# Three whole sums of squares split into two rounded products each, and an earlier wait for the first query transfers

## The chip, the cores and the metric

The kernel runs on one core of one Trainium2 chip. The time is the device time of one execution in microseconds (us), from launch to completion, and the figure used is the median of several runs. One further execution was taken with the hardware profiler: it gives each engine's instructions in time. The engines named here are TensorE (PE, matrix products; its weight loads are listed as PEld), VectorE (DVE), ScalarE (ACT), GpSimd (POOL) and SyncE (SP, which issues nearly all transfers).

## The reference, cut to what matters

Two layers work on a sequence of 512 tokens of width 1024. The first is a gated short convolution with an MLP, the second is attention with a forget gate and an MLP. The change touches the attention layer, where every key head and every query head (64 wide) is divided by its root mean square.

```python
def rms_norm(x, g):
    xf = x.astype(jnp.float32)
    y = xf * lax.rsqrt(jnp.mean(xf * xf, axis=-1, keepdims=True) + EPS)
    return y.astype(x.dtype) * g

def shared_kv(x, kv_norm_g, w_kv, k_norm_g, w_f, b_f):
    h = rms_norm(x, kv_norm_g)
    k, v = jnp.split(h @ w_kv, 2, axis=-1)
    k = rms_norm(k.reshape(b, s, N_HEADS, HEAD_DIM), k_norm_g)
    ...

def fox_mixer(h, q_w, q_norm_g, o_w, k, v, F):
    q = rms_norm((h @ q_w).reshape(b, s, N_HEADS, HEAD_DIM), q_norm_g)
    ...
        logits = jnp.einsum("bqhd,bkhd->bhqk", qb, k).astype(jnp.float32) * scale
        logits = logits + (Fq[..., :, None] - F[..., None, :])
        ...
        p = jax.nn.softmax(logits, axis=-1)
        return jnp.einsum("bhqk,bkhd->bqhd", p.astype(v.dtype), v)
```

## The kernel before

**Tiles and formats.** Activations lie with the features on the 128 partitions and the 512 tokens along the row. Keys, values and queries come in eight blocks of 128 features each (two heads per block), named k0 to k7, v0 to v7 and q0 to q7. A product with dense weights is made of three: each operand is split into a rounded part (`_hi`, type fp32r) and the rest (`_lo`), and hi·hi, lo·hi and hi·lo are added in one bank (lines 609 to 611). One block is 8 such triples over the 8 input tiles. ACT writes the rounded part of each weight block (`w_hi`, line 1117), DVE the rest (`w_lo`, line 1543). `after_block` queues both steps for the weight block three places further on.

**The order is written out by hand.** Each engine has its own list of calls, and semaphores tie them together. On every engine an instruction that waits holds up all behind it. The blocks come in the order k0, v0, k1, q0, q1, v1, and from then on k, q, v of each further number. PE alternates pieces of blocks (`kvq`) with the sums of squares (`head_sum`), the turns of values (`v_turn`), and the steps of attention: `logits`, `turn_probs`, `output`.

**The norm of one head block**, for example of k1, runs over three engines:

1. ACT, `head_square`: squares the finished bank into `tb` (line 1379), in slot 1, for q0 in slot 0.
2. PE, `head_sum`: a product with `ones_head` gives the mean over 64 features. For the blocks in `WHOLE_SQUARES` (k0, q0, k1, q1) it is one product of the whole float32 square, which the profile shows as two instructions (line 915). For all others ACT first writes a rounded copy `sq_hi` (line 1383), DVE writes the rest `sq_lo` over the square (`square_low`, line 2002), and PE multiplies the two parts (lines 918 and 920).
3. ACT, `head_root`: three activations (lines 1395 to 1397) on the sum.
4. DVE, `head_norm`: three instructions (lines 1988, 1996, 1997). The first reads the sum's bank and signals `hn_read`, the third writes the normed block `ty` and signals `normed`.
5. ACT `high` and DVE `low` split it into `qk` (lines 1402 and 2007), and SP copies that to `keys` or `queries` (line 457), from where `logits` reads.

**What else stands nearby.** The sums of k0, k1 and q1 and the turned values of block 0 share bank 3, so PE waits for `hn_read` of k1 before it starts the sum of q1. ACT's list after the first key block is: `high` of k0, square of k1, weights, square of q0, `v_high(0)` (line 1416, rounded values), root of q0, `high` of q0, root of k1, square of q1, two weight blocks, and the exponentials of head 0. DVE's list there is: norm of k0, rest of four query input tiles (`g_lo`, line 1590), weights, `low` of k0, `v_low(0)`, weights, norm of q0, `low` of q0, norm of k1, two weight blocks, and the maxima of head 0.

## Time and profile before

| | us |
|---|---|
| median of 3 runs | 1198.12 |
| lowest and highest | 1197.79, 1198.91 |
| the profiled execution, device time | 1198.92 |
| its span, first to last instruction | 1197.1 |
| PE busy in that span | 1179.0 (98%) |
| DVE busy | 763.2 (64%) |
| ACT busy | 499.5 (42%) |

The profile lists instructions with start and duration, and in brackets the idle time before one and what ended it. Matmuls are pipelined, so a matmul's listed duration is longer than the distance to the next one; what it costs PE is read from the distance between starts. The granted clock of PE is 0.999 of full speed over the span. The part that the change touches lies between about 589 and 637 us.

### The profile page before, as it was taken

How to read it: one execution, taken by the hardware profiler on the slowest of the kernel's cores; microseconds unless marked ns; L12 is line 12 of the kernel's file. 1: busy time of each engine (PE TensorE's matmuls, PEld its weight loads, DVE VectorE, ACT ScalarE, POOL GpSimd, SP SyncE). 2: the span in 40 equal slices, each digit the busy share in tenths (PEclk: the TensorE clock that was granted, in tenths of full speed). 3: DMA queues.
4: the chain of work that ended last, by engine and by line, in shares of the span. 5: the costliest groups of instructions: out<-in, count | busy, mean ns of one | idle time of the engine just before them, and what ended most of it. 6: DMA issues, size and time to landing. Idle time of an engine off the chain costs nothing.

```text
span 1197.1 us, 17104 instructions
## 1 busy us (share of the span) xinstructions
PE 1179.0 (98%) x5899; PEld 989.9 (83%) x5899; DVE 763.2 (64%) x1119; ACT 499.5 (42%) x815; POOL 24.4 (2%) x37
## 2 busy tenths in 40 slices
PE   6999999999999999999999999999999999999998
PEld 4788889888888888889978888889888888888887
DVE  5656888875665665555979898986743443443442
ACT  5422332542332332333767778864531331331431
POOL 2000000000000000002010000000000000000000
PEclk9999999999999999999999999999999999999999
DMA  9767654576666565332355544441333333333333
GB/s 335 230 194 245 189 177 132 156 237 192 187 206 196 174 200 166 88 91 71 89 141 136 130 107 124 122 127 52 90 90 103 90 104 89 104 91 101 91 102 89
DMA packets 228642, 168.77 MB, mean 141 GB/s; under 512 B 5636, under 2 KB 210604, under 8 KB 228588
## 3 DMA queue, kind: packets, MB, share of 16 engines
q1 hardware_dynamic: 228396, 167.92, 48.0%
q8 instruction: 34, 0.56, 0.2%
q0 software_dynamic: 32, 0.07, 0.0%
q14 instruction: 20, 0.16, 0.0%
q10 hardware_dynamic: 160, 0.06, 0.0%
HBM read 153.24 MB, written 2.10 MB: 130 GB/s over the span
## 4 chain that ended last, share of the span: by engine, by line
PE 90%; DVE 6%; ACT 1%; issue 1%; SPq 1%; DMA 1%; DVEq 0%; ACTq 0%
PE bank L609 28%; PE bank L611 28%; PE bank L610 28%; PE bank L956 1%; PE bank L974 1%; PE bank L707 1%; PE bank L946 1%; DVE w_lo L1543 1%; DMA first_raw<-in_sc_w_in 1%; PE bank L947 1%; DVE neg_max L2022 1%; SPq L385 1%; PE bank L737 0%; DVE h_lo L1592 0%; DVE probs L2035 0%
## 5 line engine op out<-in xcount | busy, mean ns | idle before, releaser
L609 PE MATMUL bank<-h_hi,w_hi 128*128 128x512 f32 (+1 forms) x864 | 326.2, 378 | 2.0 <-issue 1.1
L611 PE MATMUL bank<-h_hi,w_lo 128*128 128x512 f32 (+1 forms) x864 | 322.7, 373 | 0.0
L610 PE MATMUL bank<-h_lo,w_hi 128*128 128x512 f32 (+1 forms) x864 | 322.6, 373 | 0.0
L1117 ACT ACTIVATE w_hi<-raw 128x1024 fp32r<-128x1024 f32 x184 | 193.3, 1054 | 259.6 <-DMA raw<-in_mlp_w 222.3
L609 PE MATMUL bank<-g_hi,w_hi 128*128 128x512 f32 (+1 forms) x696 | 261.8, 376 | 0.0
L611 PE MATMUL bank<-g_hi,w_lo 128*128 128x512 f32 (+1 forms) x696 | 259.2, 372 | 0.0
L610 PE MATMUL bank<-g_lo,w_hi 128*128 128x512 f32 (+1 forms) x696 | 259.0, 372 | 0.0
L1543 DVE TENSOR_TENSOR w_lo<-raw,w_hi 128x1024 fp32r<-128x1024 f32 x184 | 224.7, 1224 | 45.7 <-ACT w_hi L1117 42.7
L609 PEld LDWEIGHTS bank<-h_hi,w_hi 128*128 128x128 f32 x864 | 162.6, 188 | 32.7 <-issue 3.2
L610 PEld LDWEIGHTS bank<-h_lo,w_hi 128*128 128x128 f32 x864 | 162.7, 188 | 28.7 <-issue 0.5
L611 PEld LDWEIGHTS bank<-h_hi,w_lo 128*128 128x128 f32 x864 | 162.6, 188 | 28.8
L610 PEld LDWEIGHTS bank<-g_lo,w_hi 128*128 128x128 f32 x696 | 131.2, 188 | 23.1 <-issue 0.5
L611 PEld LDWEIGHTS bank<-g_hi,w_lo 128*128 128x128 f32 x696 | 131.1, 188 | 22.9
L609 PEld LDWEIGHTS bank<-g_hi,w_hi 128*128 128x128 f32 x696 | 131.1, 188 | 22.6 <-issue 0.5
L1851 DVE SCALAR_TENSOR_TENSOR x<-bank,mod,x 128x512 f32 (+1 forms) x63 | 47.2, 750 | 141.1 <-PE bank L611 139.7
L1903 DVE TENSOR_TENSOR tb<-ta 128x512 f32<-128x512 f32 x64 | 44.3, 691 | 127.6 <-ACT ta L1319 127.6
L1319 ACT ACTIVATE ta<-bank 128x512 f32<-128x512 f32 x64 | 38.2, 596 | 195.8 <-PE bank L611 195.8
L1806 DVE SCALAR_TENSOR_TENSOR ada_acc<-ada_raw,c_act,ada_acc 128x1024 f32 (+1 forms) x80 | 102.2, 1277 | 0.6 <-DVE ada_acc L1806 0.2
L1907 DVE TENSOR_TENSOR g_lo<-tb,g_hi 128x512 f32 (+1 forms) x64 | 44.3, 693 | 15.0 <-ACT g_hi L1321 12.4
L1321 ACT ACTIVATE g_hi<-ta 128x512 f32 x64 | 40.5, 634 | 8.1
L1428 ACT ACTIVATE probs<-bank,neg_max 128x512 f32<-128x512 f32 (+1 forms) x64 | 32.9, 525 | 21.8 <-DVE neg_max L2022 21.1
L1138 ACT ACTIVATE tb<-x 128x512 f32<-128x512 f32 x15 | 9.5, 632 | 55.5 <-DVE x L1851 49.7
(225 smaller groups left out, 1072.1 us busy)
## 6 DMA issues: line engine op xcount, KB each, us to landing
raw<-in_mlp_w SPq DMA_DIRECT2D x128, 512.0 KB, 4.1
ada_raw<-in_ada_w SPq DMA_DIRECT2D x40, 1024.0 KB, 5.6
raw<-in_sc_w_in SPq DMA_DIRECT2D x20, 512.0 KB, 4.4
ada_first<-in_ada_w SPq DMA_DIRECT2D x32, 256.0 KB, 7.9
raw<-in_w_kv SPq DMA_DIRECT2D x16, 512.0 KB, 3.9
raw<-in_sc_w_out SPq DMA_DIRECT2D x8, 512.0 KB, 3.9
raw<-in_q_w SPq DMA_DIRECT2D x8, 512.0 KB, 4.7
keys<-qk SPq DMA_DIRECT2D x16, 256.0 KB, 3.1
```

Source lines behind the costliest of these rows:

```text
L609: mm(out[:, cols], weights_hi, hi[:, k, cols], start=(k == 0), stop=False)
L610: mm(out[:, cols], weights_hi, lo[:, k, cols], start=False, stop=False)
L611: return mm(out[:, cols], weights_lo, hi[:, k, cols], start=False, stop=(k == KT - 1))
L1117: go(w_hi[:, jj, :, :], raw[:, jj, :, :], ACT.Copy).then_inc(hi_ok, 1)
L1319: go(ta[:, jj % 2, :], bank[jj][:], ACT.Relu).then_inc(bank_free, 1)
L1321: go(tile3(g_hi, j), ta[:, jj % 2, :], ACT.Square).then_inc(g_hi_ok, 1)
L1428: go(probs[:, P_OFF[qt]:P_OFF[qt] + n], bank[at_bank][:, c0:c0 + n], ACT.Exp, bias=neg_max[:, s:s + 1], accum_out=p_sum[:, s:s + 1]).then_ ...
L1543: tt(w_lo[:, jj, :, :], raw[:, jj, :, :], w_hi[:, jj, :, :], ALU.subtract).then_inc(lo_ok, 1)
L1806: stt(out=acc, in0=ada_raw[:, s, half * D:(half + 1) * D], scalar=col(c_act, k), in1=acc, op0=ALU.mult, op1=ALU.add).then_inc(ada_used, 1)
L1851: stt(out=tile3(x, j), in0=bank[jj][:], scalar=mcol(layer, part, j), in1=tile3(x, j), op0=ALU.mult, op1=ALU.add).then_inc(bank_free, 1)
L1903: tt(tb[:, s, :], ta[:, s, :], ta[:, s, :], ALU.mult).then_inc(g_a, 1)
L1907: tt(tile3(g_lo, j), tb[:, s, :], tile3(g_hi, j), ALU.subtract).then_inc(g_ok, 1)
```

## The change

Only q0 stays in `WHOLE_SQUARES`. The squares of k0, k1 and q1 are now split as all later ones: ACT writes a rounded copy, DVE the rest, PE multiplies two parts. The copy of k0 goes to a new place, `first_sq_hi` in slot 0 of `tb`, as the usual place still holds query input; so the copy of the values into that slot waits for the sum of k0. The sum of k0 moves on PE from inside block v0 to its end. On ACT `v_high(0)` moves ahead of the square of q0, and in the last pair of the loop all four exponentials of head 13 stand ahead of `high` of q7, where before two stood ahead and two behind. On SP the first copy of each query half waits for the rounded part (`q_hi_ok`) alone; only the second copy waits for the rest (`q_ok`).

```diff
@@ -71,7 +71,7 @@
 SUM_BANK["q", 0] = 5
 SUM_BANK.update({("q", j): 7 for j in range(2, KT)})
 SQUARE_SLOT = {name: 0 if name == ("q", 0) else 1 for name in KVQ_ORDER}
-WHOLE_SQUARES = (("k", 0), ("q", 0), ("k", 1), ("q", 1))
+WHOLE_SQUARES = (("q", 0),)
 PARTS_OF = {name: n for n, name in enumerate(name for name in NORM_ORDER if name not in WHOLE_SQUARES)}
 
 
@@ -171,6 +171,7 @@
     qk, = stacked(region_qk, [("qk", [P, 2, 2, T], F32R)])
     region_tb = region(size([P, 2, T], F32))
     tb, = stacked(region_tb, [("tb", [P, 2, T], F32)])
+    first_sq_hi, = stacked(region_tb, [("first_sq_hi", [P, T], F32R)])
     sq_lo, = stacked(region_tb + size([P, T], F32), [("sq_lo", [P, T], F32R)])
     region_tc = region(size([P, 2, T], F32))
     tc, = stacked(region_tc, [("tc", [P, 2, T], F32)])
@@ -206,6 +207,9 @@
     def mcol(layer, part, j):
         k = (layer * NMOD + part) * KT
         return mod[:, k + j:k + j + 1] if isinstance(j, int) else mod[:, bass.ds(j + k, 1)]
+
+    def high_square(kind, j):
+        return first_sq_hi[:] if (kind, j) == ("k", 0) else sq_hi[:]
 
     def kv_gain(j):
         return cols[:, R_KV + j:R_KV + j + 1]
@@ -478,10 +482,11 @@
             def head_queries(j, half):
 
                 own, other, h = OWN[half], OWN[1 - half], 2 * j + half
-                sp.wait_ge(q_ok, j + 1)
+                sp.wait_ge(q_hi_ok, j + 1)
                 if j:
                     sp.wait_ge(s_ok, TT * (h - 1))
                 copy(queries[own, :, half, :], qk[own, 0:1, 0, :].broadcast_to([HD, 2, T])).then_inc(queries_in[half], 16)
+                sp.wait_ge(q_ok, j + 1)
                 copy(queries[other, 0, half, :], qk[own, 1, 0, :]).then_inc(queries_in[half], 16)
 
             def rest_of_pair(j):
@@ -915,7 +920,7 @@
                     mm(out, ones_head[:].bitcast(F32), tb[:, SQUARE_SLOT[kind, j], :], start=True, stop=True).then_inc(hn_pe, 1)
                 else:
                     pe.wait_ge(hn_hi, PARTS_OF[kind, j] + 1)
-                    mm(out, ones_head[:], sq_hi[:], start=True, stop=False)
+                    mm(out, ones_head[:], high_square(kind, j), start=True, stop=False)
                     pe.wait_ge(hn_lo, PARTS_OF[kind, j] + 1)
                     mm(out, ones_head[:], sq_lo[:], start=False, stop=True).then_inc(hn_pe, 1)
 
@@ -988,9 +993,8 @@
                                 block_target(KVQ, bank[KVQ_BANK["k", 0]])], 2,
                          (BLOCK_OF["v", 0], bank[KVQ_BANK["v", 0]]))
             pe.wait_ge(bank_free, KVQ)
-            kvq("v", 0, range(0, 6), cols=HALF[1])
+            kvq("v", 0, range(KT), cols=HALF[1])
             head_sum("k", 0)
-            kvq("v", 0, range(6, KT), cols=HALF[1])
             kvq("k", 1, range(KT))
             pe.wait_ge(fg_act, 2)
             kvq("q", 0, EARLY, lambda k: pe.wait_ge(h_ok, H_Q + k + 1))
@@ -1379,8 +1383,9 @@
                 go(tb[:, SQUARE_SLOT[kind, j], :], bank[KVQ_BANK[kind, j]][:], ACT.Square).then_inc(hn_sq, 1)
                 if (kind, j) not in WHOLE_SQUARES:
                     act.wait_ge(hn_sq, SQUARE_OF[kind, j] + 1)
-                    act.wait_ge(hn_pe, NORM_OF[kind, j])
-                    go(sq_hi[:], tb[:, SQUARE_SLOT[kind, j], :], ACT.Copy).then_inc(hn_hi, 1)
+                    if (kind, j) != ("k", 0):
+                        act.wait_ge(hn_pe, NORM_OF[kind, j] if (kind, j) != ("k", 1) else NORM_OF["k", 0] + 1)
+                    go(high_square(kind, j), tb[:, SQUARE_SLOT[kind, j], :], ACT.Copy).then_inc(hn_hi, 1)
 
             def root_of(kind):
                 return (tc[:, 0, :], ty[:, 0, :]) if kind == "q" else (tv[:], ty[:, 1, :])
@@ -1403,8 +1408,8 @@
 
             def v_copy(j):
                 act.wait_ge(pe_done, BLOCK_OF["v", j] + 1)
-                if j == 1:
-                    act.wait_ge(hn_pe, NORM_OF["q", 0] + 1)
+                if j < 2:
+                    act.wait_ge(hn_pe, NORM_OF["kq"[j], 0] + 1)
                 if j:
                     act.wait_ge(v_turned, j)
                 go(tb[:, 0, :], bank[KVQ_BANK["v", j]][:], ACT.Copy).then_inc(v_copied, 1)
@@ -1466,8 +1471,8 @@
             high("k", 0)
             head_square("k", 1)
             after_block("k", 1)
+            v_high(0)
             head_square("q", 0)
-            v_high(0)
             head_root("q", 0)
             high("q", 0)
             head_root("k", 1)
@@ -1498,9 +1503,10 @@
                 after_block("q", nxt)
                 head_root("q", nxt)
                 v_copy(nxt)
-                exponentials(2 * i + 1, 0, 2)
+                exponentials(2 * i + 1, 0, 2 if nxt < KT - 1 else TT)
                 high("q", nxt)
-                exponentials(2 * i + 1, 2, TT)
+                if nxt < KT - 1:
+                    exponentials(2 * i + 1, 2, TT)
                 out_high(2 * i)
                 if nxt < KT - 1:
                     head_square("k", nxt + 1)
@@ -1999,7 +2005,7 @@
 
             def square_low(kind, j):
                 dve.wait_ge(hn_hi, PARTS_OF[kind, j] + 1)
-                tt(sq_lo[:], tb[:, 1, :], sq_hi[:], ALU.subtract).then_inc(hn_lo, 1)
+                tt(sq_lo[:], tb[:, 1, :], high_square(kind, j), ALU.subtract).then_inc(hn_lo, 1)
 
             def low(kind, j):
                 n = "qk".index(kind)
@@ -2057,6 +2063,7 @@
             query_tile(2)
             query_low(1)
             query_tile(3)
+            square_low("k", 0)
             query_low(2)
             query_low(3)
             after_block("k", 0)
@@ -2071,11 +2078,13 @@
                 query_low(j)
             after_block("v", 0)
             low("k", 0)
+            square_low("k", 1)
             v_low(0)
             after_block("k", 1)
             head_norm("q", 0)
             low("q", 0)
             head_norm("k", 1)
+            square_low("q", 1)
             after_block("q", 0)
             after_block("q", 1)
             maxima(0)
```

ACT, from `high` of k0 on (`qk`) to the root of q0 (`bank5`); `tb<-bank7` is the square of k1, `tb<-bank0` that of q0, and `v_parts` is `v_high(0)`. Before:

```order
L1402 ACTIVATE qk_91<-ty_90 128x512
L1379 ACTIVATE tb_92<-bank7 128x512
L1117 ACTIVATE w_hi_82<-raw_83 128x1024
L1379 ACTIVATE tb_92<-bank0 128x512
L1416 ACTIVATE v_parts_103<-bank3 128x4x2x64
L1395 ACTIVATE ty_90<-bank5,eps_col_115 128x512
```

The same place after the change:

```order
L1407 ACTIVATE qk_91<-ty_90 128x512
L1383 ACTIVATE tb_92<-bank7 128x512
L1388 ACTIVATE sq_hi_96<-tb_92 128x512
L1121 ACTIVATE w_hi_82<-raw_83 128x1024
L1421 ACTIVATE v_parts_104<-bank3 128x4x2x64
L1383 ACTIVATE tb_92<-bank0 128x512
L1400 ACTIVATE ty_90<-bank5,eps_col_116 128x512
```

Two instructions have come in ahead of the square of q0: the rounded copy of k1's square, and the rounded values, which stood behind it.

DVE, from the last instruction of q0's norm to the maxima of head 0. Before:

```order
L1997 SCALAR_TENSOR_TENSOR ty_90<-bank0,q_gain_113,ssum_88 128x512
L2007 TENSOR_TENSOR qk_91<-ty_90,qk_91 128x512
L1988 SCALAR_TENSOR_TENSOR ssum_88<-bank3,tv_96 128x512
L1996 SCALAR_TENSOR_TENSOR ssum_88<-ssum_88,ty_90 128x512
L1997 SCALAR_TENSOR_TENSOR ty_90<-bank7,k_gain_114,ssum_88 128x512
L1543 TENSOR_TENSOR w_lo_81<-raw_83,w_hi_82 128x1024 x2
L2022 TENSOR_REDUCE neg_max_118<-bank6 128x1
```

The same place after the change:

```order
L2003 SCALAR_TENSOR_TENSOR ty_90<-bank0,q_gain_114,ssum_88 128x512
L2013 TENSOR_TENSOR qk_91<-ty_90,qk_91 128x512
L1994 SCALAR_TENSOR_TENSOR ssum_88<-bank3,tv_97 128x512
L2002 SCALAR_TENSOR_TENSOR ssum_88<-ssum_88,ty_90 128x512
L2003 SCALAR_TENSOR_TENSOR ty_90<-bank7,k_gain_115,ssum_88 128x512
L2008 TENSOR_TENSOR sq_lo_94<-tb_92,sq_hi_96 128x512
L1549 TENSOR_TENSOR w_lo_81<-raw_83,w_hi_82 128x1024 x2
L2028 TENSOR_REDUCE neg_max_119<-bank6 128x1
```

The rest of q1's square (`sq_lo`) stands behind all three instructions of k1's norm.

PE, the sum of q1 inside block v1 (`bank0`) and the start of the first logits (`mask_b`). Before:

```order
L611 MATMUL bank0<-h_hi_50,w_lo_81 128x512
L915 MATMUL bank3<-tb_92,ones_head_100 128x512
L609 MATMUL bank0<-h_hi_50,w_hi_82 128x512
L610 MATMUL bank0<-h_lo_51,w_hi_82 128x512
L611 MATMUL bank0<-h_hi_50,w_lo_81 128x512
L936 MATMUL bank6<-mask_b_102,ident_b_101 128x128
```

The same place after the change:

```order
L616 MATMUL bank0<-h_hi_50,w_lo_81 128x512
L923 MATMUL bank3<-sq_hi_96,ones_head_101 128x512
L925 MATMUL bank3<-sq_lo_94,ones_head_101 128x512
L614 MATMUL bank0<-h_hi_50,w_hi_82 128x512
L615 MATMUL bank0<-h_lo_51,w_hi_82 128x512
L616 MATMUL bank0<-h_hi_50,w_lo_81 128x512
L941 MATMUL bank6<-mask_b_103,ident_b_102 128x128
```

The sum stands at the same place, now as two products, of which the second needs DVE's `sq_lo`.

## Rows read from the trace of the kernel before

**Rows 1.** The page: the chain of waits that ended last, by engine

```profile
PE 90%; DVE 6%; ACT 1%; issue 1%; SPq 1%; DMA 1%; DVEq 0%; ACTq 0%
```

**Rows 2.** Chain of waits in order of time, sums of squares: start, us, what

```profile
591.51 0.86 PE bank L915 x2
...
609.02 0.86 PE bank L915 x2
...
660.80 0.23 PE bank L918
```

**Rows 3.** Timeline of ACT, `high` of k0 to `v_high(0)`: start, duration, what

```profile
601.16 0.63 ACT L1402 ACTIVATE qk<-ty 128x512 fp32r<-128x512 f32 x1 [1.21 <-DVE g_lo L1590]
601.69 0.58 ACT L1379 ACTIVATE tb<-bank 128x512 f32<-128x512 f32 x1
602.17 1.05 ACT L1117 ACTIVATE w_hi<-raw 128x1024 fp32r<-128x1024 f32 x1
604.51 0.60 ACT L1379 ACTIVATE tb<-bank 128x512 f32<-128x512 f32 x1 [1.28 <-PE bank L611]
605.00 0.59 ACT L1416 ACTIVATE v_parts<-bank 128x512 fp32r<-128x512 f32 x1
```

**Rows 4.** Timeline of ACT, the square of k2 with its rounded copy

```profile
630.09 0.58 ACT L1379 ACTIVATE tb<-bank 128x512 f32<-128x512 f32 x1
630.70 0.63 ACT L1383 ACTIVATE sq_hi<-tb 128x512 fp32r<-128x512 f32 x1
631.23 0.57 ACT L1446 ACTIVATE o_hi<-bank 64x512 fp32r<-64x512 f32 x1
```

**Rows 5.** Timeline of PE, the sum of q0 and the product ahead of it

```profile
604.76 0.39 PE L611 MATMUL bank<-g_hi,w_lo 128*128 128x512 f32 x1
605.16 1.12 PE L915 MATMUL bank<-tb,ones_head 128*128 128x512 f32 x2
```

**Rows 6.** Timeline of DVE, the norm of k1 to the maxima of head 0

```profile
613.18 0.69 DVE L1988 SCALAR_TENSOR_TENSOR ssum<-bank,tv 128x512 f32<-128x512 f32 x1 [1.21 <-ACT tv L1397]
613.91 0.69 DVE L1996 SCALAR_TENSOR_TENSOR ssum<-ssum,ty 128x512 f32<-128x512 f32 x1
614.64 0.75 DVE L1997 SCALAR_TENSOR_TENSOR ty<-bank,k_gain,ssum 128x512 f32<-128x512 f32 x1
615.31 2.35 DVE L1543 TENSOR_TENSOR w_lo<-raw,w_hi 128x1024 fp32r<-128x1024 f32 x2
617.57 1.67 DVE L2022 TENSOR_REDUCE neg_max<-bank 128x1 f32<-128x512 f32 x4
```

**Rows 7.** Timeline of DVE, the rest of the square of k2 and what follows

```profile
631.61 0.68 DVE L2002 TENSOR_TENSOR sq_lo<-tb,sq_hi 128x512 fp32r<-128x512 f32 x1
632.22 0.68 DVE L2049 TENSOR_TENSOR o_lo<-bank,o_hi 64x512 fp32r<-64x512 f32 x1
```

**Rows 8.** Timeline of PE, the sum of q1 to the first logits

```profile
613.62 0.39 PE L611 MATMUL bank<-h_hi,w_lo 128*128 128x512 f32 x1
613.93 1.12 PE L915 MATMUL bank<-tb,ones_head 128*128 128x512 f32 x2
...
615.12 0.40 PE L610 MATMUL bank<-h_lo,w_hi 128*128 128x512 f32 x1
...
615.60 0.40 PE L936 MATMUL bank<-mask_b,ident_b 128*128 128x128 bf16 x4
616.11 0.47 PE L946 MATMUL bank<-keys,queries 128*128 128x512 f32 x1
```

**Rows 9.** Timeline of SP, the copies of the first queries: issue, duration, what

```profile
612.00 2.74 SPq L457 DMA_DIRECT2D queries<-qk  x4
```

**Rows 10.** Stretches: length, PE busy (instructions), granted clock, DMA share, GB/s

```profile
20.00:24.00 4.00, 3.45 (x16) 0.69 1.08 361
24.00:28.00 4.00, 4.00 (x21) 0.88 1.11 349
```

**Rows 11.** Timeline of PE, the product after the longest wait between products

```profile
20.55 1.06 PE L727 MATMUL bank<-ident,x_unit 128*128 128x128 f32 x8 [1.78 <-ACT tc L1224]
```

## The prediction, on record before the changed kernel ran

> **What bounds the kernel now.** I read the chain of waits first. PE has 90% of it and DVE 6% [rows 1], so time is won or lost where PE's list gets shorter or where PE has to wait. The change touches only the stretch from the first key block to the first logits, and one place near the end of attention. For that stretch I then read the timelines of PE, ACT, DVE and SP side by side. The reader is to see three things. The sums of squares stand in an unbroken row of products, so a shorter sum is time won if its inputs are there [rows 2]. ACT is idle for 1.21 and 1.28 us just ahead of the steps that feed q0's sum [rows 3], which is room for added work, but not for all of it. And the sum of q1 already starts late, since PE waits for the first instruction of k1's norm, with two more of that norm behind it on DVE [rows 6, 8].
>
> **What the split sums save on PE.** In an unbroken row the float32 sum costs 0.86 us (k0 and k1) and one rounded product 0.23 [rows 2]. Two of these are 0.46, so each of k0, k1 and q1 saves 0.40 to 0.41, in all 1.2 us. After an idle moment the float32 pair costs more: from 613.93 to 615.12 less the 0.23 of the one product between, 0.96 [rows 8]. Moving k0's sum from inside v0 to its end adds no product.
>
> The row says that a float32 product costs 0.86/0.23 = 3.7 rounded ones. The Trainium skill (FP8 and Floating Point Precision, TensorE Precision Notes) counts four passes through the array for true float32. By four passes the three sums would save 0.46 each, 1.4 us in all, against the 1.2 by the rows.
>
> **k0: the added work is covered, but it pushes ACT and DVE.** A square with its copy takes ACT 631.23 − 630.09 = 1.14 us, a square alone 602.17 − 601.69 = 0.48 [rows 3, 4], so each copy adds 0.66 to ACT's list. Each `sq_lo` adds 632.22 − 631.61 = 0.61 to DVE's [rows 7]. The sum of k0 now stands some 0.7 us later on PE, where copy and rest are done. But ACT and DVE have no pause from there to `high` of k0, which waits for DVE's `g_lo` [rows 3]. DVE in turn waits for ACT's root of k0. So `high` of k0 starts 0.66 later, at 601.82; PE does not wait for it.
>
> **q0: ACT's backlog reaches the sum.** From 601.82 on ACT runs `high`, the square of k1, its copy (0.66 again), a weight block and now `v_high(0)`. The weight block starts at 602.17 + 0.66 + 0.66 = 603.49 and passes the engine on 0.95 later (an instruction starts about 0.1 before the listed end of the last one), at 604.44. `v_high(0)` takes 0.49, taken from the distance 604.51 to 605.00 of the square there [rows 3]. The square of q0 starts at 604.93 and lasts 0.60, to 605.53. With the 0.05 from square to product of before (604.51 + 0.60 = 605.11, then 605.16) the sum of q0 starts at 605.58 [rows 3, 5]. Before, it started at 605.16, after a wait of 605.16 − (604.76 + 0.23) = 0.17 [rows 5]. PE, 0.41 earlier through k0, would be ready at 604.58, so the wait grows from 0.17 to 1.0: **+0.83**. The move of `v_high` costs 0.49 of that: without the copies it would fit into the idle 1.28, with them it does not. The gain of k0 is gone, and PE stands 0.42 later than before.
>
> **k1.** Its copy ends near 603.6 (601.82, then 0.53 for `high`, 0.61 for the square, 0.63 for the copy), and its `sq_lo` follows on DVE. PE comes to the sum at 605.58 + 0.96 + 4 tiles of three products (2.7) = 609.3, so the parts are long there. So its 0.41 is won, and PE is level with before (613.8) when it comes to the sum of q1.
>
> **q1: a new wait.** Between the sum of q0 and that of q1 runs a chain that the change leaves as it is: root of q0 on ACT, norm of q0 on DVE, `high` of q0 and root of k1 on ACT, first instruction of k1's norm on DVE. It took 613.93 − 605.16 = 8.77 us [rows 5, 8]. So PE may start the sum of q1 at 605.58 + 8.77 = 614.35. The first product needs ACT's copy. The second needs `sq_lo`, and on DVE that stands behind the second and third instruction of k1's norm. Before, the instruction in that place (the weights) started at 615.31 [rows 6]; 0.42 later is 615.73, and with 0.68 for the subtraction [rows 7] it ends at 616.41. PE goes on at 616.45 and is through at 616.68. Before it was through at 615.12 − 0.23 = 614.89 [rows 8]. **PE is 1.8 us behind here**, of which 1.46 is pure waiting between the two products. Queued behind the second product are the rest of v1 and the logits of head 0; no other engine has work that would shorten this. Behind `sq_lo` on DVE stand two weight blocks and the maxima of head 0. These were not waiting for PE before (DVE came without a pause, at 617.57 [rows 6]); they come about 1.0 later (0.42 + 0.61), and PE's logits 1.5 later, so DVE adds nothing.
>
> **Queries.** Four products of 128 columns need about 0.23, so before the first logits PE waited (616.11 − 615.60) − 0.23 = 0.28 [rows 8], most likely for the query copies issued from 612.00 [rows 9]. Now the first copy needs only the rounded part, which comes 0.42 later but spares the rest (0.68): the copies go out about 0.3 earlier, and PE comes 1.8 later. The wait goes: **−0.3**. For later blocks I take zero: the copies land while PE has other work. Bounds: −0.3 to 0.
>
> **The last pair.** Head 13's last two exponentials now stand ahead of `high` of q7. On ACT that place was idle, waiting for DVE's norm of q7, and DVE's own order is unchanged, so I take zero. No row tells it better; by one exponential and half a wait the bounds are −0.4 to +0.4.
>
> **Sum against the profiled span.** −0.41 (k0) + 0.83 (q0) − 0.41 (k1) + 1.8 (q1, with its own saving) − 0.3 (queries) = +1.5 us, so the span goes from 1197.1 to 1198.6. After the first logits PE is the bound again and carries this to the end. The profiled execution took 1198.92, 0.8 above the median; against the median, 1198.12 + 1.5 = 1199.6.
>
> **Rivals.**
>
> *Cover holds.* If the parts of q1's square are there when PE comes, and q0's square is on time, only savings are left: −1.23, the waits of 0.17 ahead of q0 and 0.08 ahead of q1 (613.93 − 613.62 − 0.23) [rows 8], and 0.28 for the queries, −1.7: 1196.4. For it: the room of 1.21 and 1.28 on ACT [rows 3]. Against it: DVE's order, in which `sq_lo` of q1 cannot start before k1's norm is over. Chance 0.10.
>
> *q0 on time, q1 late.* If ACT catches up by the square of q0 (less than 0.5 of backlog), PE comes to it as early as it can. Square and sum then start 0.41 earlier than before, and all of the q1 chain with them: 0.8 less than my forecast, +0.7, 1198.8. Chance 0.15.
>
> *The clock falls (slower).* After its longest wait between products, 1.78 us with one-column products ahead of it, PE's granted clock was 0.69 in 20 to 24 and 0.88 in 24 to 28 [rows 10, 11]. That is 4 × 0.31 + 4 × 0.12 = 1.7 us lost at the 1.2 GHz level. The change makes PE idle for nearly all of 614.0 to 616.45, with one product in it. If that is enough, the loss is 1.5 + 1.7 = 3.2: 1201.3. It decides when the wait at q1 is at least as long as the one at 20 us. Against it: the products right before and after are full 512-column ones. Chance 0.17.
>
> The Trainium skill (TensorE: Matmul & The Clock Gate, HAM oscillation) tells of the same fall after idle gaps between bursts of products. The trace agrees once, in the rows just named.
>
> *It does nothing.* If savings and waits cancel, the time is 1198.1. I count that between the second rival and the forecast, chance 0.03.
>
> **How the numbers follow.** The forecast, 1199.0 to 1200.4 with the bounds of the small terms, has 0.55. With the second rival and the clock the range 1197.8 to 1201.6 holds about 0.87; what is left out is the case of cover and accidents. About 0.2% (2.4 us) is what a measurement of this kernel can tell from no change. Faster than 1195.7 needs more than every saving together: 0.03. Slower than 1200.5 needs the clock or the upper end of the forecast: 0.17 + 0.06 = 0.23. The rest is within 0.2%: 0.74.
>
> **What would show it.** In the changed profile: two products of 0.23 at k0 with no idle before them; the square of q0 on ACT starting at 604.9 without idle before it; the sum of q0 at 605.6; q1's second product more than 1.5 us behind the first, with DVE's `sq_lo` as releaser; first logits near 617.6; clock 1.00 from 612 to 620. I am wrong if ACT is idle ahead of q0's square, if DVE does `sq_lo` of q1 before k1's norm ends, or if waits after 620 us shrink and give the 1.5 back.

## The result: 1200.9 us, 0.2% slower than before

| | us |
|---|---|
| before, median of 20 runs beside the changed kernel | 1198.24 (1197.50 to 1200.03) |
| after, median of 20 runs | 1200.90 (1199.43 to 1202.64) |
| after / before, with 95% interval | 1.0023 [1.0017, 1.0029] |
| after, span of the profiled execution | 1200.8 |

The kernel became 2.7 us slower, where 1.5 was forecast. The 20 runs are spread wide, and their mean granted clocks tell why in part: 7 runs have a mean clock of 0.996 and take 1201.95 to 1202.64 (median 1202.53). The other 13 have 0.997 to 0.999 and a median of 1200.42. Of 87 runs of the kernel before, taken beside this kernel's experiments, none has a mean clock of 0.996. The profiled execution of after is one of the 7. Its span is 3.7 longer than that of before.

Of these 3.7, about 0.6 arose before anything that the change touches. ACT's square of k0 starts at 589.39 before and at 589.96 after. In the profiled executions of this case it lies anywhere between 588.25 and 589.96. A part of that goes with the granted clock near the start, which in 16 to 28 us is 0.72 in some executions (after and five others: square at 589.24 to 589.96) and 0.86 in the rest (before and six others: 588.25 to 589.39). Where single times of after are compared with before, I take off 0.58 (instructions ahead of the change start 0.57 to 0.59 apart). For whole stretches I count from that square of k0.

**k0 and k1.** The sums cost PE what two rounded products cost in a row, without an idle moment. This timeline of PE (start, duration, what, and in brackets the idle time before it and what ended it) answers to the first two of [rows 2]:

```profile
592.63 0.40 PE L923 MATMUL bank<-first_sq_hi,ones_head 128*128 128x512 f32 x1
592.87 0.40 PE L925 MATMUL bank<-sq_lo,ones_head 128*128 128x512 f32 x1
593.10 0.39 PE L614 MATMUL bank<-h_hi,w_hi 128*128 128x512 f32 x1
...
609.86 0.39 PE L923 MATMUL bank<-sq_hi,ones_head 128*128 128x512 f32 x1
610.09 0.39 PE L925 MATMUL bank<-sq_lo,ones_head 128*128 128x512 f32 x1
```

From 592.63 to 593.10 are 0.47, and at k1 the two are 0.23 apart, 0.46 for both. Before it was 0.86 each.

**q0.** ACT has no pause between `high` of k0 and the square of q0, and PE waits for that square. First ACT, as [rows 3], then PE, as [rows 5]:

```profile
602.40 0.63 ACT L1407 ACTIVATE qk<-ty 128x512 fp32r<-128x512 f32 x1 [1.21 <-DVE g_lo L1596]
602.94 0.58 ACT L1383 ACTIVATE tb<-bank 128x512 f32<-128x512 f32 x1
603.55 0.63 ACT L1388 ACTIVATE sq_hi<-tb 128x512 fp32r<-128x512 f32 x1
604.09 1.05 ACT L1121 ACTIVATE w_hi<-raw 128x1024 fp32r<-128x1024 f32 x1
605.04 0.58 ACT L1421 ACTIVATE v_parts<-bank 128x512 fp32r<-128x512 f32 x1
605.51 0.59 ACT L1383 ACTIVATE tb<-bank 128x512 f32<-128x512 f32 x1
```

```profile
604.93 0.39 PE L616 MATMUL bank<-g_hi,w_lo 128*128 128x512 f32 x1
606.15 1.13 PE L920 MATMUL bank<-tb,ones_head 128*128 128x512 f32 x2 [0.84 <-ACT tb L1383]
```

The product ahead is through at 604.93 + 0.23 = 605.16, so the wait is 0.99, where [rows 5] give 0.17.

**q1.** PE waits twice. The timeline of PE answers to [rows 8]:

```profile
614.17 0.39 PE L616 MATMUL bank<-h_hi,w_lo 128*128 128x512 f32 x1
615.45 0.47 PE L923 MATMUL bank<-sq_hi,ones_head 128*128 128x512 f32 x1 [0.90 <-ACT sq_hi L1388]
617.05 0.80 PE L925 MATMUL bank<-sq_lo,ones_head 128*128 128x512 f32 x1 [1.13 <-DVE sq_lo L2008]
617.64 0.63 PE L614 MATMUL bank<-h_hi,w_hi 128*128 128x512 f32 x1
618.07 0.63 PE L615 MATMUL bank<-h_lo,w_hi 128*128 128x512 f32 x1
...
618.93 0.65 PE L941 MATMUL bank<-mask_b,ident_b 128*128 128x128 bf16 x4
619.34 0.78 PE L951 MATMUL bank<-keys,queries 128*128 128x512 f32 x1
```

The waits are 1.05 ahead of the first product and nearly all of the 1.60 between the two. On DVE the rest of the square stands where the prediction put it, behind the whole norm of k1 (as [rows 6]):

```profile
614.19 0.69 DVE L1994 SCALAR_TENSOR_TENSOR ssum<-bank,tv 128x512 f32<-128x512 f32 x1 [1.21 <-ACT tv L1402]
...
615.65 0.75 DVE L2003 SCALAR_TENSOR_TENSOR ty<-bank,k_gain,ssum 128x512 f32<-128x512 f32 x1
616.32 0.68 DVE L2008 TENSOR_TENSOR sq_lo<-tb,sq_hi 128x512 fp32r<-128x512 f32 x1
616.91 2.35 DVE L1549 TENSOR_TENSOR w_lo<-raw,w_hi 128x1024 fp32r<-128x1024 f32 x2
620.49 1.68 DVE L2028 TENSOR_REDUCE neg_max<-bank 128x1 f32<-128x512 f32 x4 [1.23 <-PE bank L952]
```

**The clock.** From 617.64 on the products stand 0.43 apart instead of 0.23. The granted clock in stretches of 1 us (length, PE busy with instructions, clock, DMA share, GB/s) shows it:

```profile
616.00:617.00 1.00, 0.00 (x0) 0.91 0.99 245
617.00:618.00 1.00, 0.95 (x2) 0.50 0.65 180
618.00:619.00 1.00, 1.00 (x4) 0.50 1.10 334
619.00:620.00 1.00, 1.00 (x7) 0.50 0.14 42
620.00:621.00 1.00, 1.00 (x7) 0.89 0.00 0
```

0.50 is the 1.2 GHz level. Near the end of the second wait, the clock fell, and it was back some 3.4 us later (finer stretches give 0.53 for 616.8 to 617.0, 0.50 from there to 620.2, and 0.94 for the 0.2 us behind). The 0.09 that is missing in the first row passed while PE had nothing to do, so what PE lost is 3 × 0.50 + 0.11 = 1.6 us. Before, 612 to 624 has a granted clock of 1.00.

From the square of k0 to the turn of the fourth block of probabilities there are 66.66 us before and 69.75 after: 3.1 more. Less the 1.6 for the clock, 1.5 is left for waits and savings.

### The profile page after: what moved, and what is told of

Same layout as the page of the kernel before. It is cut to its first block, busy times and chain, and to the rows that moved or that the text cites. A ratio compares the mean times of both kernels' runs of the same rounds, so it can differ in the third digit from the quotient of the medians.

```text
span 1200.8 us, 17113 instructions
## 1 busy us (share of the span) xinstructions
PE 1179.6 (98%) x5899; PEld 991.8 (83%) x5899; DVE 765.4 (64%) x1122; ACT 501.7 (42%) x818; POOL 24.7 (2%) x37
## 4 chain that ended last, share of the span: by engine, by line
PE 90%; DVE 5%; ACT 2%; issue 1%; SPq 1%; DMA 1%; DVEq 0%; ACTq 0%
PE bank L614 28%; PE bank L616 27%; PE bank L615 27%; PE bank L961 1%; PE bank L979 1%; PE bank L951 1%; PE bank L952 1%; PE bank L712 1%; DMA first_raw<-in_sc_w_in 1%; SPq L389 1%; DVE h_lo L1598 0%; DVE w_lo L1549 0%; PE bank L742 0%; DVE tc L1589 0%; DVE x L1628 0%
```

## The experiments

Each was run 11 times beside 27 to 33 runs of the kernel before (medians 1198.31, 1198.34 and 1198.31), except the queries alone, which have one execution. The stretch is that from ACT's square of k0 to the turn of the fourth block of probabilities in the profiled execution; it leaves the start-up out. Before it is 66.66, after 69.75. The ratio is an estimate over all runs, nearer to that of the means than to that of the medians. A ratio whose interval holds 1 can't be told from no change.

| edit on the changed kernel | median us | ratio [95%] | stretch | runs at clock 0.996 |
|---|---|---|---|---|
| none | 1200.90 | 1.0023 [1.0017, 1.0029] | 69.75 | 7 of 20 |
| q1 whole again | 1198.79 | 1.0003 [0.9994, 1.0012] | 66.98 | 0 of 11 |
| idle products in the waits at q1 | 1199.88 | 1.0013 [1.0004, 1.0022] | 68.26 | 0 of 11 |
| `sq_lo` of q1 inside k1's norm | 1199.66 | 1.0012 [1.0003, 1.0021] | 68.01 | 0 of 11 |
| `v_high(0)` back | 1201.01 | 1.0017 [1.0008, 1.0026] | 69.37 | 4 of 11 |
| copy of k1 behind q0's square | 1201.60 | 1.0021 [1.0012, 1.0030] | 69.51 | 7 of 11 |
| the same with idle products | 1199.68 | 1.0011 [1.0002, 1.0020] | 67.99 | 0 of 11 |
| sum of q1 later on PE | 1199.15 | 1.0008 [0.9999, 1.0017] | 67.35 | 0 of 11 |
| several moves together | 1198.30 | 1.0001 [0.9992, 1.0010] | 66.29 | 0 of 11 |
| the same, weights later | 1197.56 | 0.9995 [0.9986, 1.0004] | 66.15 | 0 of 11 |
| k0 alone split | 1198.08 | 0.9996 [0.9987, 1.0005] | 66.13 | 0 of 11 |

### Is it q1? The sum of q1 whole again

```diff
-WHOLE_SQUARES = (("q", 0),)
+WHOLE_SQUARES = (("q", 0), ("q", 1))
...
             head_norm("k", 1)
-            square_low("q", 1)
```

> The changed kernel with one part undone: the square of q1 is summed whole again, k0 and k1 stay split. Theory (the loss is q1's wait for the rest of its square, behind k1's norm on VectorE, plus the clock that this wait brings down): the sum of q1 starts where the chain from q0's sum allows, 0.42 us later than in the kernel before, the queries' wait of 0.28 goes, so the time is 0.1 us above the kernel before, about 1198.3, and the granted clock stays at 1.00 around the first logits in every run. Rival (ScalarE's backlog ahead of q0's sum does the harm by itself, clock included): the time stays at 1199.6 or more, since that backlog is all still there.

Measured 1198.79, by its ratio not to be told from before, and far from the rival's 1199.6. The stretch is 66.98, 2.8 shorter than after's and 0.3 longer than before's. The wait for q0 is as long as in after (the product ahead starts at 603.73):

```profile
604.96 1.12 PE L920 MATMUL bank<-tb,ones_head 128*128 128x512 f32 x2 [0.84 <-ACT tb L1383]
```

So the wait at q0 is real, and k0 and k1 don't make it good: counted from the square of k0, the sum of q1 starts at 613.75 − 588.76 = 24.99, where before it was 613.93 − 589.39 = 24.54, so 0.45 later (0.42 by the prediction). The queries give 0.3 of it back. What is left is too small to be seen in the time. The loss that can be measured hangs on q1's split, with its wait and the clock behind it.

### Wait or clock? Idle products in the waits at q1

Four products whose result is never used stand ahead of the sum of q1, six between its two products. They write a bank that the logits start afresh.

```diff
+            filler(4)
             pe.wait_ge(hn_read, NORM_OF["k", 1] + 1)
             head_sum("q", 1)
...
                     mm(out, ones_head[:], high_square(kind, j), start=True, stop=False)
+                    if (kind, j) == ("q", 1):
+                        filler(6)
```

> The changed kernel with ten idle products added on TensorE (512 columns each, into a bank that is free there, result not used): four ahead of the wait for the sum of q1, six between its two products. They take 0.92 and 1.38 us and fit into the waits of 0.5 to 0.9 and 1.4 us, so no later instruction is released later by more than 0.1. Theory (waits cost 1.5 us; in a part of the runs the clock falls to 1.2 GHz for 3.4 us because TensorE idles, and that costs 1.6 more): the clock stays at 1.00 from 612 to 624 us, all runs lie in one group, median about 1199.7. Rival (the clock does not matter and the waits or something later cost the whole 2.7): the median stays at 1200.9 and runs spread from 1199.4 to 1202.6 as those of the changed kernel did.

Measured 1199.88, with the stretch at 68.26, +1.60 against before. The first of q1's two products comes when it did in after, the second 0.1 later (27.20 against 27.09 behind the square of k0), but the clock stays up. The two rows show 612 to 616 and 616 to 620 of this kernel, then the same of after (columns as above):

```profile
612.00:616.00 4.00, 4.00 (x18) 1.00 0.86 200
616.00:620.00 4.00, 4.00 (x24) 1.00 0.45 128
```

```profile
612.00:616.00 4.00, 3.03 (x13) 1.00 0.58 129
616.00:620.00 4.00, 2.95 (x10) 0.60 0.72 200
```

With PE kept busy there is no fall and no run at 0.996. So the fall comes from PE's idling at q1. What stays without it, +1.6 with the 0.1 of the idle products in it, is the price of the waits less the savings, where +1.5 was forecast.

### The rest of q1's square earlier on DVE

```diff
-            head_norm("k", 1)
-            square_low("q", 1)
+            head_read("k", 1)
+            square_low("q", 1)
+            head_scale("k", 1)
```

`head_read` is the first instruction of the norm, `head_scale` the other two.

> The changed kernel with one VectorE instruction moved: the rest of q1's square stands right behind the first instruction of k1's norm instead of behind all three. Theory (order on VectorE makes the wait between q1's two products): the subtraction starts when ScalarE's copy is done, 614.7 on the scale of the kernel before, ends at 615.4, TensorE is through the sum at 615.7 instead of 616.7, 1.0 us won, and the idle time is short enough that the clock seldom falls: median 1198.6 to 1199.2. k1's norm ends 0.7 later, which nothing waits for. Rival (the wait is set by ScalarE's copy or its backlog): no more than 0.3 us won against the changed kernel, 1200.5 or more.

Measured 1199.66; I had expected up to 1199.2. PE's wait between the two products falls from 1.37 to 615.07 − 614.43 − 0.23 = 0.41, but a new one stands before the first turn of probabilities:

```profile
615.07 0.50 PE L925 MATMUL bank<-sq_lo,ones_head 128*128 128x512 f32 x1 [0.16 <-DVE sq_lo L2008]
...
621.54 0.39 PE L616 MATMUL bank<-h_hi,w_lo 128*128 128x512 f32 x1
622.40 0.77 PE L961 MATMUL bank<-ident,probs 128*128 128x128 f32 x5 [0.47 <-DVE probs L2041]
```

DVE explains it. The maxima follow its two weight blocks without a pause, at 618.58, which is 29.65 after this execution's square of k0 (588.93). Before it was 617.57 − 589.39 = 28.18 [rows 6]. So the maxima come 1.5 late and set the start of the softmax: 0.45 through the start of k1's norm, 0.45 because `sq_lo` now waits for ACT's copy in front of the rest of the norm, 0.6 for `sq_lo` itself.

```profile
614.32 0.69 DVE L2008 TENSOR_TENSOR sq_lo<-tb,sq_hi 128x512 fp32r<-128x512 f32 x1 [0.45 <-ACT sq_hi L1388]
...
616.31 2.35 DVE L1549 TENSOR_TENSOR w_lo<-raw,w_hi 128x1024 fp32r<-128x1024 f32 x2
618.58 1.68 DVE L2028 TENSOR_REDUCE neg_max<-bank 128x1 f32<-128x512 f32 x4
```

The wait of 622.40 − 621.54 − 0.23 = 0.63 gives back part of what was won. What I had left out is DVE's own list: in after it is 1.0 late at its weights, which does not show behind PE's longer waits, and the edit made that 1.5.

### The wait at q0: two edits on ACT's list

First the values go back behind the square of q0:

```diff
-            v_high(0)
             head_square("q", 0)
+            v_high(0)
```

> The changed kernel with ScalarE's rounding of the values of block 0 moved back behind the square of q0. Theory (each ScalarE instruction ahead of the square of q0 delays its sum and all of the chain to the sum of q1): the sum of q0 and that of q1 come 0.49 us earlier, TensorE is 1.0 instead of 1.5 us behind the kernel before in runs with a full clock, and the wait between q1's products stays at 1.4, so the clock still falls in some runs: median 1199.8 to 1200.6, fastest runs 0.5 below those of the changed kernel (1198.9). Rival (the move is free, as ScalarE was idle there before): within 0.1 us of the changed kernel, 1200.9.

```profile
604.39 0.39 PE L616 MATMUL bank<-g_hi,w_lo 128*128 128x512 f32 x1
605.13 1.12 PE L920 MATMUL bank<-tb,ones_head 128*128 128x512 f32 x2 [0.35 <-ACT tb L1383]
```

The wait fell from 0.99 to 0.51. The 0.48 won is the 0.49 by which the prediction priced the move of `v_high`. The stretch followed by 0.38. The median, 1201.01, did not show it, against at most 1200.6 expected: four of 11 runs have the mean clock of 0.996 (median 1201.6), the rest a median of 1199.95, and how many of each there are moves the median by more than the edit.

Then k1's rounded copy goes behind the square of q0 too, and ACT is early for q0:

```diff
             high("k", 0)
             head_square("k", 1)
             after_block("k", 1)
-            v_high(0)
             head_square("q", 0)
+            square_high("k", 1)
+            v_high(0)
```

Here `head_square` no longer makes k1's copy; `square_high` does.

> The changed kernel with two ScalarE instructions moved behind the square of q0: the rounded copy of k1's square, and the rounding of the values of block 0. Theory (ScalarE's added work ahead of q0's square makes q0's wait and shifts the whole chain to q1's sum): ScalarE is idle again before the square of q0, TensorE waits 0.2 us there instead of 1.0, and every later step up to the sum of q1 comes 0.8 us earlier than in the changed kernel. The wait between q1's products stays at 1.4, so the clock still falls in some runs: fastest runs 0.8 below those of the changed kernel, about 1198.6, median 1199.0 to 1200.2. Rival (q0's wait is made good later, so its size does not matter): fastest runs as those of the changed kernel, 1199.4, median 1200.9.

The wait at q0 is back at before's 0.17 (604.21 to 604.61), yet the median is 1201.60, against at most 1200.2 expected and above the rival's 1200.9 too, and 7 of 11 runs have the clock of 0.996. The sum of q1 shows what happened:

```profile
612.65 0.39 PE L616 MATMUL bank<-h_hi,w_lo 128*128 128x512 f32 x1
614.43 0.47 PE L923 MATMUL bank<-sq_hi,ones_head 128*128 128x512 f32 x1 [1.40 <-ACT sq_hi L1392]
616.03 0.79 PE L925 MATMUL bank<-sq_lo,ones_head 128*128 128x512 f32 x1 [1.13 <-DVE sq_lo L2013]
```

In 616 to 620 the granted clock of this execution is 0.57. Counted from the square of k0, PE came 0.8 earlier to the sum of q1 than in after, but ACT's copy only 0.3 earlier, so the wait ahead of the first product grew from 1.05 to 1.55. The chain lost the 0.5 because an instruction of q0's norm took longer on DVE, 1.24 where the same one takes 0.71 in after. First this kernel, then after:

```profile
608.55 1.24 DVE L2007 SCALAR_TENSOR_TENSOR ssum<-ssum,ty 128x512 f32<-128x512 f32 x1
```

```profile
610.09 0.71 DVE L2002 SCALAR_TENSOR_TENSOR ssum<-ssum,ty 128x512 f32<-128x512 f32 x1
```

GpSimd was at work on the forget gate then. So of the 0.8 taken away at q0, 0.5 came back at q1, where PE is now idle for longer in one place. Whether that is why the clock fell more often (7 of 11 against 7 of 20) so few runs can't say.

The same kernel with the idle products of the second experiment tells how much of it is the clock:

```diff
+            filler(4)
             pe.wait_ge(hn_read, NORM_OF["k", 1] + 1)
```

> e5_k1_copy_late with the ten idle products of e2_fill. In e5_k1_copy_late the waits in the stretch were shorter than in the changed kernel, but 7 of 11 executions lay above 1201.3 with a mean clock of 0.996. Theory (the wait at q1's sum brings down the clock and that costs 1.7): clock 1.00 from 612 to 624, no execution above 1201, median 1199.1, and the stretch from k0's square to the fourth turn 67.8 instead of 69.5. Rival (the slow executions have another cause than idle time on TensorE): some executions above 1201.3 remain.

```profile
616.00:620.00 4.00, 4.00 (x25) 1.00 0.45 130
```

Measured 1199.68, 1.9 below the kernel without them, and the stretch 67.99, 1.5 below. No run has 0.996. The median is 0.6 above what I had expected, the stretch 0.2. This is the second pair of kernels that differ by idle products alone, with the same outcome. The two of this pair ran on different chips, on which the kernel before had nearly the same median (1198.34 and 1198.31) and no run at 0.996. In both pairs together, 14 of 31 runs have the clock of 0.996 without idle products and none of 22 with them: PE's idling makes the clock fall.

### The sum of q1 later in PE's list

PE does five tiles of v1 ahead of the sum instead of three, and the logits follow at once. One tile of k2 moves ahead of the first turn.

```diff
-            kvq("v", 1, range(0, 3))
+            kvq("v", 1, range(0, 5))
             pe.wait_ge(hn_read, NORM_OF["k", 1] + 1)
             head_sum("q", 1)
-            kvq("v", 1, range(3, 4))
...
-            kvq("k", 2, range(0, 2))
+            kvq("k", 2, range(0, 3))
             turn_probs(0)
```

> The changed kernel with work moved only on TensorE: two more tiles of v1 stand ahead of the sum of q1 (five instead of three), the logits of head 0 follow right behind that sum, and one tile of k2 moves ahead of the first turn of probabilities. Theory (the wait at q1's sum is a matter of what TensorE has to do meanwhile): 1.36 us of products fill the wait, TensorE idles about 1.1 instead of 2.4 us there, the clock stays at 1.00 in most runs, but VectorE, 1.0 behind, makes the first turn of probabilities wait some 0.6: median 1198.6 to 1199.4. Rival (idle time is only pushed to the next place that waits for VectorE): within 0.5 of the changed kernel's runs at full clock, 1200 or more.

```profile
614.47 0.39 PE L923 MATMUL bank<-sq_hi,ones_head 128*128 128x512 f32 x1
615.75 0.50 PE L925 MATMUL bank<-sq_lo,ones_head 128*128 128x512 f32 x1 [0.90 <-DVE sq_lo L2007]
```

Measured 1199.15, within the expectation; the interval of its ratio still holds 1. The first product has its input now. The wait for DVE's `sq_lo` is 615.75 − 614.47 − 0.23 = 1.05, and with that one wait left at q1 no run has the clock of 0.996. The wait of 0.6 that I had expected before the first turn of probabilities is not there.

### The queries alone, on the kernel before (one execution)

```diff
-                sp.wait_ge(q_ok, j + 1)
+                sp.wait_ge(q_hi_ok, j + 1)
...
+                sp.wait_ge(q_ok, j + 1)
                 copy(queries[other, 0, half, :], qk[own, 1, 0, :]).then_inc(queries_in[half], 16)
```

> The kernel before with the SyncE part of the change alone: the first copy of each query half waits for the rounded part only. Theory (the 0.28 us ahead of the first logits was a wait for query copies): the distance from the first mask product to the first logits product falls from 0.51 to 0.2 us, and nothing else moves: span 0.3 us shorter, too little for one time to show. Rival (the wait was for something else): the distance stays at 0.5.

```profile
616.12 0.40 PE L937 MATMUL bank<-mask_b,ident_b 128*128 128x128 bf16 x4
616.33 0.48 PE L947 MATMUL bank<-keys,queries 128*128 128x512 f32 x1
```

From mask to first logits there are 0.21 now, the four products alone; [rows 8] have 0.51. So the 0.3 is there. At the turn of the fourth block of probabilities only 0.15 of it was left. The time of this one execution, 1199.29, can't show either.

### Can a version win?

Three were tried. The first takes together: copy of k1 late, the sum of q1 later on PE, `sq_lo` of q1 inside k1's norm, and on DVE weights and maxima in another order. In DVE's list:

```diff
-            square_low("k", 1)
-            v_low(0)
             after_block("k", 1)
+            square_low("k", 1)
+            v_low(0)
             head_norm("q", 0)
...
             after_block("q", 0)
-            after_block("q", 1)
             maxima(0)
             normalize(0)
+            after_block("q", 1)
             low("k", 1)
```

> All orders changed together, the same split sums as in the changed kernel: on ScalarE k1's copy and the values behind q0's square; on VectorE the rest of q1's square behind the first instruction of k1's norm, v1's weights ahead of the rest of k1's square, and the maxima and the normalizing of head 0 ahead of q2's weights; on TensorE the order with two more tiles of v1 ahead of q1's sum. Theory (the split sums save 1.3 us on TensorE if no part comes late): no wait above 0.3 us in 600 to 625, clock 1.00, 1.2 to 1.7 us below the kernel before: median 1196.6 to 1197.1. Rival (VectorE and ScalarE have no room for three more splits, so some wait always takes the place of the saving): within 0.5 of the kernel before, 1197.8 to 1198.8.

Measured 1198.30, no faster than before. In its stretch of 66.29 the large waits at q0 and q1 are gone, but PE comes early enough to wait 0.3 before the first logits again (615.78 − 615.25 − 0.23), in spite of the earlier query copies, and a new wait of 0.64 stands ahead of the second head's logits, since DVE's `pt_lo` is behind the weights that were moved:

```profile
623.50 0.40 PE L616 MATMUL bank<-h_hi,w_lo 128*128 128x512 f32 x1
624.37 0.40 PE L941 MATMUL bank<-mask_b,ident_b 128*128 128x128 bf16 x4 [0.47 <-DVE pt_lo L2052]
```

The second puts those weights behind `probs_low(0)`:

```diff
             low("k", 1)
             probs_low(0)
+            after_block("q", 1)
```

> As e7_best, but VectorE's part of q2's weights stands behind the rest of head 0's turned probabilities instead of ahead of it. In e7_best TensorE waited 0.65 us for those probabilities before the logits of head 1. Theory (that instruction's place gave back half of the saving): the wait goes, the stretch from k0's square to the fourth turn of probabilities, 66.66 us in the kernel before and 66.29 in e7_best, falls to 65.6 to 65.8, and the time to 0.9 us below the kernel before, 1197.4. Rival (VectorE is full there, so the wait turns up at the logits of head 1 or at the next turn): stretch 66.2 or more, time as before.

Measured 1197.56, ratio 0.9995 [0.9986, 1.0004]: it can't be told from before. Its wait at that place is 0.47 instead of 0.64, where I had expected it to go, and the stretch is 66.15, close to the rival's 66.2.

The third keeps the split for k0 alone, with `v_high(0)` back in its old place:

```diff
-WHOLE_SQUARES = (("q", 0),)
+WHOLE_SQUARES = (("q", 0), ("k", 1), ("q", 1))
```

> The changed kernel with only k0's square split; k1 and q1 are summed whole again, and the rounding of the values of block 0 stands behind q0's square. Theory (ScalarE has 1.28 us to spare ahead of q0's square, and one copy of 0.66 fits): the sum of q0 starts 0.4 us earlier than in the kernel before and takes the chain up to q1's sum with it, the queries' wait goes; stretch from k0's square to the fourth turn 66.0 (before 66.66), no wait above 0.3 us, time 0.7 below the kernel before, 1197.6. Rival (even one added split on ScalarE and VectorE eats its 0.41): stretch 66.5 or more.

Its stretch is 66.13, 0.5 below before's, with the sum of q0 0.4 earlier as expected (15.37 behind the square of k0 against 15.77). The time, 1198.08 with a ratio of 0.9996 [0.9987, 1.0005], can't show that.

## Why the prediction was right in kind and short in size

**k0 and k1: right.** 0.47 and 0.46 instead of 0.86, with no idle before the first product.

**q0: right.** Forecast: square of q0 at 604.93, sum at 605.58, a wait of 1.0. Measured, less the 0.58: 604.93, 605.57, 0.99. The 0.49 for the move of `v_high` came out as 0.48 when it was undone.

**q1: right in place and size of the waits.** Forecast: second product at 616.45. Measured: 617.05 − 0.58 = 616.47, with `sq_lo` as releaser. The first came at 614.87 where the prediction had 614.35 as the earliest, so the 0.5 lay in the wait for ACT's copy (L1388) rather than in that for DVE. That changes nothing in the sum, since the second product ends last. What the prediction calls 1.46 of pure waiting between the products is by its own times 616.45 − 614.35 − 0.23 = 1.87, of which 1.46 is left after the saving of 0.41; the 1.8 of the sum does not rest on it. Both waits together were to be 2.42 by its times (from 613.8 to 616.45 less one product), and 1.05 + 1.37 = 2.42 were measured.

**DVE behind it: right for this kernel.** In after the maxima wait for PE (1.23), as forecast. Where PE came earlier, in the third experiment, DVE set the time.

**Queries: right for this kernel.** −0.3 was forecast and 0.30 seen when that edit was made alone. Where PE comes earlier, as in the first of the three versions, the wait of 0.3 is back. In after, mask to logits is 0.41 at half clock, which is no wait either. SP issues the queries at 612.29 − 0.58 = 611.71, 0.3 earlier than in [rows 9].

**The last pair: right.** The wait before the turn of head 13 is 787.70 − 786.87 − 0.23 = 0.60; at the same place of the kernel before it is 0.61.

```profile
786.87 0.39 PE L616 MATMUL bank<-o_hi,w_lo 128*128 128x512 f32 x1
787.70 0.98 PE L961 MATMUL bank<-ident,probs 128*128 128x128 f32 x7 [0.45 <-DVE probs L2041]
```

**The sum: +1.5 forecast, +1.6 measured with the clock held up** (stretch and median of the kernel with idle products agree within 0.1), and of that 0.1 is the idle products' own.

**The clock: the term that was mis-sized.** It stood at zero in the sum, as a rival of 1.7 us with a chance of 0.17 and the note that full products around the wait speak against it. They don't help: the fall came, for 1.6 us, in the profiled execution and, by the mean clock, in about a third of the runs. It came with waits of 1.05 and 1.37, both shorter than the 1.78 that the rival asked for. "If that is enough" had no yes or no as its answer, but a share of executions. The 7 runs at 0.996 lift the median from 1200.42 (the other 13) to 1200.90, which lies above the range of 1199.0 to 1200.4 that the prediction gives its forecast, and inside the wide one of 1197.8 to 1201.6. That is luck in part: the 7 take 1202.5, so with the fall in most of the runs the median would have left the wide range too.

The mean clock marks the fall only roughly. The three profiled executions at 0.996 have both the fall at q1 and the long fall of the start-up. The start-up alone makes 0.9 us of difference in the kernel before (29 runs at 0.997 with a median of 1198.88, 43 at 0.999 with 1197.97), so the 2.1 between the two groups of after are not all the price of q1's fall. And a fall at q1 behind the short start-up would read about 0.997. After has three such runs, and they take no longer than those at 0.999 (1200.33 to 1200.86), which speaks against it.

**What stays open.** The 13 other runs are 2.2 above before, not 1.5. Nine have a mean clock of 0.999, which leaves no room for a second fall of this size beside the one of the start-up, and their median is 1200.42 too. The two variants with the fall don't show such a rest clearly: their other runs are 1.6 and 1.2 above before (7 and 4 runs). The trace shows one execution only, and that is one of the others. What the 0.7 is made of, I can't say.

## What to carry to other kernels

Splitting one step into two that are fed by two engines can make PE wait for the later of them: read, on each feeding engine, what stands ahead of the new instruction before counting the saving on PE. A wait of PE can have a second price, the clock behind it, which is to be added as a share of executions, and it can be measured by itself with idle products in the wait. Taking a wait away pays as far as the chain behind it keeps its length: of 0.48 won at q0 by the move of `v_high` the stretch kept 0.38, of 0.8 won there with the copy of k1 moved as well it kept 0.24, since an instruction of the chain took 0.53 longer.

## What the runs showed of the hardware that I had not expected

**A fall of the clock in some executions of a kernel and not in others.** In after PE idled 1.05 and 1.37 us (617.05 − 615.45 − 0.23) with one 512-column product between, in the midst of full products at 1.00. The clock then read 0.50 for some 3.4 us. By the mean clock that happened in 7 of 20 runs of after, 4 of 11 and 7 of 11 of two variants, and in none of the kernels whose waits were filled or shorter. In the three profiled executions with a fall at q1 the clock of the start-up was also at its lower value (0.72 in 16 to 28). The three other profiled executions with 0.72 are of kernels without these waits, and no execution with both the waits and a start-up of 0.86 was profiled, so whether the two falls go together stays open. The Trainium skill (TensorE: Matmul & The Clock Gate, Part 1: The HAM clock gate) notes that the point at which the clock rises differs from run to run of one kernel. The runs here show as much for a fall: it comes in some executions of a kernel and not in others.

**DVE instructions with two inputs can get longer beside GpSimd.** The 128x512 instruction in q0's norm took 1.24 instead of 0.71, and `sq_lo` of k1 in the first of the three versions tried took 1.47, against 0.68 for the same form elsewhere [rows 7]. GpSimd ran its forget-gate instructions during both, as the timelines of that version show for the second, first DVE, then GpSimd:

```profile
605.23 1.47 DVE L2012 TENSOR_TENSOR sq_lo<-tb,sq_hi 128x512 fp32r<-128x512 f32 x1
```

```profile
604.06 2.09 POOL L603 TENSOR_TENSOR fg_u<-fg_f,neg_f 16x512 f32<-16x512 f32 x1
```

The Trainium skill (GPSIMD Engine Reference, Specifications) says that the two engines share interfaces to SBUF and contend when a DVE instruction has two inputs there. These rows fit that; no experiment took GpSimd's work away to show it. Nor does every overlap hit DVE: in the kernel with the copy of k1 behind q0's square, DVE's weights (606.32, line 1554) keep their 1.22 beside a GpSimd conversion (606.33), and it is that one which takes 1.67 instead of 0.60 before.
